# Scores of the two components side by side on the row halves of TensorE, masks behind both

## The chip, the cores and the metric

The kernel runs on one core of a Trainium2 chip. The metric is the device time of one execution in microseconds. Times of single instructions come from one profiled execution of the same program.

## The reference, cut to what matters

Two transformer blocks are computed one after the other, all in fp32, with 512 tokens and a width of 1024. The change touches only the first attention of the first block, a differential attention with 8 heads. Each head has two components of 64 features for queries and keys, and one value of 128 features:

```python
def one_block(args):                      # qblk: 128 queries, i: their block
    qblk, i = args
    s = jnp.einsum('bqhcd,bkhcd->bhcqk', qblk, k) * scale      # c: the 2 components
    causal = kpos[None, :] <= qpos[:, None]
    p = jax.nn.softmax(jnp.where(causal, s, NEG_INF), axis=-1)
    a = p[:, :, 0] - lam * p[:, :, 1]
    return jnp.einsum('bhqk,bkhe->bqhe', a, v)
```

Everything behind it (output projection, feed-forward layers, a windowed attention, a block of convolutions, another attention) is the same code before and after.

## The kernel before, in words

Each engine has its own program; they meet at counting semaphores. The first attention is the stage `heads`. It goes over 8 heads, and within a head over 4 slots, one for each block i of 128 queries. Because of the causal mask, slot i looks at n = 128 (i + 1) keys: 128, 256, 384 and 512.

In a slot TensorE does, in this order (function `slot`, L2145):

1. `scores` (L2106): for each component c one fp32 matmul of the 128 queries against n keys. Its operands stand in `da_T`, component 0 in partitions 0 to 63, component 1 in partitions 64 to 127, so that each matmul uses one half of the array's rows. It writes PSUM bank 2 + c. Behind it a bf16 matmul of the identity with a mask adds -1e30 to the part of the diagonal block that lies above the diagonal, and tells VectorE (`sc`). This one uses all 128 rows.
2. `turn` (L2122): transposes of the attention weights of the slot before, which wait for VectorE's `combine` (`comb`). In slot 3 also `turn_outputs`.
3. `project` (L2084): 24 matmuls of 384 columns, the projection of one token tile of the next head. In slot 0 it waits for that head's low weight halves (`s_lo`), which VectorE makes in `refill`.
4. `values` (L2131): the weights of the slot before times v, when ScalarE has copied them (`ate`).
5. `turn_qk` (L2098): transposes of queries and keys of one token tile, which wait for VectorE's `rope`.

VectorE goes through a slot in a fixed order: the negated row maximum of either component (`sc` to `mx`, L1685), in slot 1 the head's outputs, then `rope` of one tile of the next head (L1628 to L1634), in slots 2 and 3 more of the output's normalization, `combine` (L1643 to L1648), and last `refill` (L1675): one piece of the weights of the head after the next in slot 3, and two pieces in slot 0. ScalarE takes the exponentials (L988) behind the maxima, copies the turned weights, makes the high weight halves, and empties the projections out of PSUM.

The last head has no projection of a next head; TensorE fills its slots with steps of the output projection (L1950 to L1952), for which ScalarE (L763) and VectorE (L1305) split the weights.

Of the kernel before, what the change touches and what calls it, by code (L numbers as in the profile page):

```python
# [15 lines left out]
P = 128  # L16
D = 1024
KT_D = D // P
SEQ = 512
CTX = 256  # L20
ALL = SEQ + CTX
HD = 64
# [156 lines left out]
def program(nc, dram, out):  # L179
    stages = make_plan()  # L180
    stack = ExitStack()
    with stack:
# [3 lines left out]
        def sem(name):  # L186
            return stack.enter_context(nc.semaphore(name))
# [85 lines left out]
        pb = psum[:].rearrange("p (b n) -> p b n", b=8)  # L273
# [16 lines left out]
        s_mm = sem("block_multiplied")  # L290
# [1656 lines left out]
        def _(pe):  # L1947
# [133 lines left out]
            def heads(st):  # L2081
                S = s_da
# [23 lines left out]
                def scores(h, par, i, first):  # L2106
                    n = (i + 1) * P
                    pe.wait_ge(S["qte"], 4 * h + (i + 1))
                    qT = da_T[:, par, :]
                    for c in range(2):  # L2110
                        u = 2 * i + c
                        if not (first and i == 0):
                            pe.wait_ge(S["ex"], 8 * h + (u - 1))
                        rows_ = slice(HD * c, HD * c + HD)
                        r = pe.matmul(pb[:, 2 + c, 0:n], qT[rows_, i * P:(i + 1) * P], qT[rows_, SEQ:SEQ + n],  # L2115
                                      start=True, stop=False)
                        if u == 0:
                            r.then_inc(s_mm, 1)
                        pe.matmul(pb[:, 2 + c, i * P:n], ident_b[:], masks_b[:, 1, :], start=False, stop=True)\
                          .then_inc(S["sc"], 1)  # L2120

# [23 lines left out]
                def slot(h, par, i, first=False, more=True):  # L2145
                    j = 4 * h + i
                    scores(h, par, i, first)
                    if not more:
                        pair(st["after"], *((0, 1), (2, 3), (4, 5), (5, 6))[i])
                    if not (first and i == 0):  # L2150
                        turn(j - 1, (i - 1) % 4)
                    if not more and i < 2:
                        pair(st["after"], 2 * i + 1, 2 * i + 2)
                    if i == 3 and not first:
                        pe.wait_ge(S["qte"], j + 3 if more else 32)
                        turn_outputs(h - 1)
                    if first and i < 3:
                        project(i + 5, i + 1, 1, 1)
                    if first and i == 0:
                        turn_qk(1, 1)  # L2160
                        turn_qk(2, 2)
                    if more and not first:
                        project(j + 4, i, 1 - par, h + 1)
                    if not (first and i == 0):
                        if i == 1 and not first:
                            pe.wait_ge(S["osb"], h)
                        values(j - 1, par if i else 1 - par, (i - 1) % 4)
                    if i == 3 and not first and more:
                        pe.wait_ge(S["olo"], h)
                    if i == 0:  # L2170
                        turn_qk(j + 3, 3)
                    elif more:
                        turn_qk(j + 3, i - 1)

                for k in range(KT_D):
# [6 lines left out]
                    for t in range(4):  # L2182
# [4 lines left out]
                        r = pe.matmul(dst, xl, wh, start=False, stop=k == KT_D - 1)  # L2187
# [344 lines left out]
```

## Time and profile before

| | us |
|---|---|
| median of 3 runs | 2894.89 (2893.93 to 2895.11) |
| profiled execution, its time | 2899.06 |
| profiled execution, its span | 2897.1 |
| TensorE busy in the span | 2783.3 (96%) |
| VectorE busy | 1777.8 (61%) |
| ScalarE busy | 1115.3 (38%) |

The stage `heads` has its first scores at 41.5 us and its last at about 263.7 us. From the second head on a head takes 28.78 us. The share of busy time is one over stages with different limits, so the stage is read from its timeline. A busy TensorE also holds time in which it drains: the ends of its matmuls are modelled, and the distance from one start to the next is the surer number.

### The profile page before, as it was taken

To read this page: it belongs to the slowest core of one execution; us is meant where nothing else is said; L and a number is where in the kernel's file an instruction comes from. 1 tells how busy PE (TensorE), PEld (TensorE's weight loads), DVE (VectorE), ACT (ScalarE), POOL (GpSimd) and SP (SyncE) were. 2 spreads that over 40 slices of the span, in tenths; PEclk is the share of its full clock that TensorE was granted. 3 is DMA by queue.
4 is the path that set the end of the run, shared out by engine and by line. 5 is a ranking of instruction groups with operands and counts; after the bars stand their busy time and mean duration, and the time that the engine had idled before them with its cause. 6 is when DMAs were issued, how large, how long until landed. Compare 5 with 4: busy or idle time off the path is not lost.

```text
span 2897.1 us, 41339 instructions
## 1 busy us (share of the span) xinstructions
PE 2783.3 (96%) x14371; PEld 2317.5 (80%) x14371; DVE 1777.8 (61%) x2765; ACT 1115.3 (38%) x1869; POOL 160.5 (6%) x205
## 2 busy tenths in 40 slices
PE   7999999999788999999998999999999999999998
PEld 6887788888676788887887888888888887788886
DVE  6775667676665676667884653453456655564645
ACT  5553322224664322223433332231224666452432
POOL 5211000001110000000210000000000000000000
PEclk9999999999999999999998999999999999999999
DMA  3211355452011455532751112112111000232322
GB/s 131 65 45 58 124 179 181 165 177 75 30 37 52 145 187 175 175 131 73 158 123 45 48 64 67 59 58 69 58 57 44 15 30 30 67 101 90 100 87 66
DMA packets 75218, 263.72 MB, mean 91 GB/s; under 512 B 8496, under 2 KB 10800, under 8 KB 73264
## 3 DMA queue, kind: packets, MB, share of 16 engines
q1 hardware_dynamic: 70880, 249.99, 25.6%
q0 software_dynamic: 4176, 11.63, 2.2%
q8 instruction: 94, 1.54, 0.2%
q14 instruction: 68, 0.56, 0.1%
HBM read 247.87 MB, written 2.10 MB: 86 GB/s over the span
## 4 chain that ended last, share of the span: by engine, by line
PE 65%; issue 15%; DVE 11%; ACT 6%; DVEq 1%; ACTq 1%; POOLq 1%; POOL 0%
PE psum L1950 17%; PE psum L1951 17%; PE psum L1952 17%; DVE w_lo L1305 2%; PE psum L2115 2%; ACT work L1107 2%; DVE work L1475 1%; PE psum L2093 1%; PE psum L2095 1%; PE psum L2094 1%; PE psum L2368 1%; ACT w_hi L763 1%; ACT sw_pt L1119 1%; DVE work L1593 1%; ACT work L814 1%
## 5 line engine op out<-in xcount | busy, mean ns | idle before, releaser
L1950 PE MATMUL psum<-hx_hi,w_hi 128*128 128x512 f32 x1568 | 624.5, 398 | 4.0 <-DVE hx_lo L1587 1.2
L1951 PE MATMUL psum<-hx_lo,w_hi 128*128 128x512 f32 x1568 | 622.0, 397 | 0.0
L1952 PE MATMUL psum<-hx_hi,w_lo 128*128 128x512 f32 x1568 | 621.3, 396 | 0.0
L763 ACT ACTIVATE w_hi<-w_raw 128x1024 fp32r<-128x1024 f32 (+1 forms) x328 | 344.7, 1051 | 511.8 <-PE psum L1952 211.5
L1305 DVE TENSOR_TENSOR w_lo<-w_raw,w_hi 128x1024 fp32r<-128x1024 f32 (+1 forms) x328 | 398.2, 1214 | 197.2 <-ACT w_hi L763 179.9
L1952 PEld LDWEIGHTS psum<-hx_hi,w_lo 128*128 128x128 f32 x1568 | 295.0, 188 | 71.9
L1950 PEld LDWEIGHTS psum<-hx_hi,w_hi 128*128 128x128 f32 x1568 | 295.3, 188 | 62.8 <-DVE hx_lo L1587 4.6
L1951 PEld LDWEIGHTS psum<-hx_lo,w_hi 128*128 128x128 f32 x1568 | 295.1, 188 | 47.5
L1950 PE MATMUL psum<-a_hi,w_hi 128*128 128x512 f32 (+1 forms) x656 | 233.9, 356 | 9.5 <-DVE a_lo L1415 8.9
L1951 PE MATMUL psum<-a_lo,w_hi 128*128 128x512 f32 (+1 forms) x656 | 233.7, 356 | 0.0
L1952 PE MATMUL psum<-a_hi,w_lo 128*128 128x512 f32 (+1 forms) x656 | 233.4, 356 | 0.0
L1950 PE MATMUL psum<-o_hi,w_hi 128*128 128x512 f32 x544 | 219.4, 403 | 1.8 <-DVE w_lo L1305 1.8
L1952 PE MATMUL psum<-o_hi,w_lo 128*128 128x512 f32 x544 | 217.2, 399 | 0.0
L1951 PE MATMUL psum<-o_lo,w_hi 128*128 128x512 f32 x544 | 217.0, 399 | 0.0
L1437 DVE SCALAR_TENSOR_TENSOR work<-psum,vec,work 128x511 f32<-128x511 f32 (+1 forms) x132 | 83.2, 658 | 167.2 <-ACT work L844 158.9
L564 POOL TENSOR_TENSOR tok_r<-tok_ms,half 128x4 f32<-128x4 f32 (+1 forms) x62 | 67.2, 1084 | 1892.9 <-DVE tok_ms L1233 1581.0
L1379 DVE SCALAR_TENSOR_TENSOR X<-psum,mods,X 128x512 f32<-128x512 f32 x96 | 60.6, 659 | 173.3 <-PE psum L1952 171.1
L844 ACT ACTIVATE work<-psum,vec 128x768 f32<-128x768 f32 (+1 forms) x88 | 70.1, 797 | 225.3 <-PE psum L1952 216.8
L1950 PEld LDWEIGHTS psum<-a_hi,w_hi 128*128 128x128 f32 x656 | 124.7, 190 | 29.5 <-DVE a_lo L1415 9.5
L1952 PE MATMUL psum<-hc_hi,w_lo 128*128 128x256 f32 x512 | 144.5, 282 | 0.0
L1950 PE MATMUL psum<-hc_hi,w_hi 128*128 128x256 f32 x512 | 144.3, 282 | 0.0
L1951 PE MATMUL psum<-hc_lo,w_hi 128*128 128x256 f32 x512 | 144.0, 281 | 0.0
(310 smaller groups left out, 4920.6 us busy)
## 6 DMA issues: line engine op xcount, KB each, us to landing
mod_w<-in_w_mod SPq DMA_DIRECT2D x96, 512.0 KB, 3.8
w_raw<-in_fup SPq DMA_DIRECT2D x88, 512.0 KB, 4.6
w_raw<-in_cup SPq DMA_DIRECT2D x88, 512.0 KB, 3.6
w_raw<-in_fdown SPq DMA_DIRECT2D x32, 512.0 KB, 4.7
w_raw<-in_cdown SPq DMA_DIRECT2D x32, 512.0 KB, 3.6
sw_vb<-tap_prod POOLq DMA_DIRECT2D x29, 391.5 KB, 5.0
w_raw<-in_da_qkv SPq DMA_DIRECT2D x18, 512.0 KB, 3.6
w_raw<-in_fdown SPq DMA_DIRECT2D x16, 384.0 KB, 3.1
```

Of the source, the lines that this page charges most:

```text
L564: pool.tensor_tensor(tok_r[:, a:b], tok_ms[:, a:b], half[:, a:b], ALU.pow).then_inc(done, 1)
L763: r = act.activation(w_hi[:, off:off + n], w_raw[:, raw:raw + n], ACT.Copy)
L814: act.activation(wk[:, s % 2, 0:n], X[:, b, 0:n], ACT.Square).then_inc(s_sq, 1)
L844: act.activation(wk[:, s, 0:toks], ps_of(st, s, 0, toks), ACT.Copy, scale=vec[:, bass.ds(b + col, 1)]).then_inc(s_ctap, 1)
L1107: r = act.activation(work[:, e:e + (w1 - w0)], psum[:, w0:w1], ACT.Exp, bias=neg_max[:, col:col + 1], scale=root, accum_out=row_sum[:, col ...
L1305: r = dve.tensor_tensor(w_lo[:, off:off + n], w_raw[:, raw:raw + n], w_hi[:, off:off + n].bitcast(F32), ALU.subtract)
L1379: r = dve.scalar_tensor_tensor(X[:, b, a:e], ps_of(st, s, a, e), mods[:, l, c, bass.ds(b + o, 1)], X[:, b, a:e], ALU.mult, ALU.add)
L1437: dve.scalar_tensor_tensor(dst[:, a + 1:e], src(a, e - 1), prev, dst[:, a + 1:e], ALU.mult, ALU.add)
L1950: pe.matmul(dst, wh, xh, start=first, stop=False)
L1951: pe.matmul(dst, wh, xl, start=False, stop=False)
L1952: return pe.matmul(dst, wl, xh, start=False, stop=last)
L2115: r = pe.matmul(pb[:, 2 + c, 0:n], qT[rows_, i * P:(i + 1) * P], qT[rows_, SEQ:SEQ + n], start=True, stop=False)
```

## The change

`scores` now issues the matmuls of both components before either mask. With 384 or 512 keys each matmul is cut into two pieces of half the width, in the order component 0, component 1, component 0, component 1. `start` is set on the first piece only, which clears the bank's flags. The two masks come behind, one after the other. The waits for `ex` stand where they stood, ahead of the first piece of each component. Nothing else changes.

```diff
                     qT = da_T[:, par, :]
+                    wide = n // 2 if i >= 2 else n
+                    for a in range(0, n, wide):
+                        for c in range(2):
+                            if a == 0 and not (first and i == 0):
+                                pe.wait_ge(S["ex"], 8 * h + (2 * i + c - 1))
+                            rows_ = slice(HD * c, HD * c + HD)
+                            r = pe.matmul(pb[:, 2 + c, a:a + wide], qT[rows_, i * P:(i + 1) * P],
+                                          qT[rows_, SEQ + a:SEQ + a + wide], start=a == 0, stop=False)
+                            if i == 0 and c == 0:
+                                r.then_inc(s_mm, 1)
                     for c in range(2):
-                        u = 2 * i + c
-                        if not (first and i == 0):
-                            pe.wait_ge(S["ex"], 8 * h + (u - 1))
-                        rows_ = slice(HD * c, HD * c + HD)
-                        r = pe.matmul(pb[:, 2 + c, 0:n], qT[rows_, i * P:(i + 1) * P], qT[rows_, SEQ:SEQ + n],
-                                      start=True, stop=False)
-                        if u == 0:
-                            r.then_inc(s_mm, 1)
                         pe.matmul(pb[:, 2 + c, i * P:n], ident_b[:], masks_b[:, 1, :], start=False, stop=True)\
                           .then_inc(S["sc"], 1)
```

## Rows read from the trace of the kernel before

**Rows 1.** The page: busy time by engine over the whole span.

```profile
PE 2783.3 (96%) x14371; PEld 2317.5 (80%) x14371; DVE 1777.8 (61%) x2765; ACT 1115.3 (38%) x1869; POOL 160.5 (6%) x205
```

**Rows 2.** Stretches: length, busy time by engine, granted TensorE clock, DMA share, GB/s.

```profile
157.24:186.02 28.78, 28.78 (x163) 24.33 (x163) 21.55 (x47) 16.39 (x49) 5.83 (x6) 1.00 0.18 55
...
260.00:275.20 15.20, 13.07 (x45) 8.74 (x45) 3.68 (x7) 3.33 (x7) 0.00 (x0) 0.66 0.00 2
```

**Rows 3.** Timeline of TensorE, slot 0 of a head: start, us, instruction.

```profile
157.17 0.49 PE L2115 MATMUL psum<-da_T 64*128 64x128 f32 x2
157.59 0.23 PE L2119 MATMUL psum<-masks_b,ident_b 128*128 128x128 bf16 x1
157.75 0.48 PE L2115 MATMUL psum<-da_T 64*128 64x128 f32 x2
158.16 0.23 PE L2119 MATMUL psum<-masks_b,ident_b 128*128 128x128 bf16 x1
158.23 0.60 PE L2128 MATMUL psum<-ident,work 128*128 128x128 f32 x4
158.59 0.42 PE L2093 MATMUL psum<-w_hi,hx_hi 128*128 128x384 f32 x1
```

**Rows 4.** Timeline of TensorE: values and transposes ahead of slot 1, then slot 1.

```profile
162.91 1.05 PE L2135 MATMUL psum<-da_v,da_aT 128*128 128x128 f32 x8
163.80 0.38 PE L2103 MATMUL psum<-ident,da_qk 128*128 128x128 f32 x2
164.11 0.70 PE L2115 MATMUL psum<-da_T 64*128 64x256 f32 x2
...
165.60 0.28 PE L2128 MATMUL psum<-ident,work 128*128 128x128 f32 x1
```

**Rows 5.** Timeline of TensorE: the end of slot 1 and the scores of slot 2.

```profile
170.17 0.38 PE L2103 MATMUL psum<-ident,da_qk 128*128 128x128 f32 x2
170.48 0.91 PE L2115 MATMUL psum<-da_T 64*128 64x384 f32 x2
...
172.39 0.39 PE L2128 MATMUL psum<-ident,work 128*128 128x128 f32 x2
```

**Rows 6.** Timeline of TensorE: the scores of slot 3.

```profile
177.62 1.12 PE L2115 MATMUL psum<-da_T 64*128 64x512 f32 x2
178.67 0.23 PE L2119 MATMUL psum<-masks_b,ident_b 128*128 128x128 bf16 x1
178.83 1.12 PE L2115 MATMUL psum<-da_T 64*128 64x512 f32 x2
...
179.95 0.50 PE L2128 MATMUL psum<-ident,work 128*128 128x128 f32 x3
```

**Rows 7.** Timeline of VectorE in slot 3, idle time before in brackets.

```profile
178.94 0.69 DVE L1685 TENSOR_REDUCE neg_max<-psum 128x1 f32<-128x512 f32 x1 [1.32 <-PE psum L2119]
180.16 0.69 DVE L1685 TENSOR_REDUCE neg_max<-psum 128x1 f32<-128x512 f32 x1 [0.52 <-PE psum L2119]
...
185.79 1.22 DVE L1675 TENSOR_TENSOR w_lo<-w_raw,w_hi 128x1024 fp32r<-128x1024 f32 x1 [0.16 <-issue]
```

**Rows 8.** Timeline of VectorE: refill in slot 3, rope in slot 1, first maximum in slot 2.

```profile
157.01 1.23 DVE L1675 TENSOR_TENSOR w_lo<-w_raw,w_hi 128x1024 fp32r<-128x1024 f32 x1 [0.16 <-issue]
...
169.01 0.42 DVE L1634 TENSOR_TENSOR da_qk<-work,tok_r 128x256 f32<-128x256 f32 x1
...
171.59 0.56 DVE L1685 TENSOR_REDUCE neg_max<-psum 128x1 f32<-128x384 f32 x1 [1.04 <-PE psum L2119]
```

**Rows 9.** Timeline of all engines in the last head, slots 2 and 3.

```profile
257.36 1.02 DVE L1685 TENSOR_REDUCE neg_max<-psum 128x1 f32<-128x384 f32 x2
...
259.51 0.71 PE L2135 MATMUL psum<-da_v,da_aT 128*128 128x128 f32 x4 [1.38 <-ACT da_aT L960]
...
260.15 1.38 PE L2115 MATMUL psum<-da_T 64*128 64x512 f32 x2
...
261.68 2.07 PE L2115 MATMUL psum<-da_T 64*128 64x512 f32 x2
```

## Prediction

> **What bounds the kernel now.** I read the page first: TensorE is busy for 96% of the span [rows 1], so the question is whether it also sets the pace where the change is, and what in its busy time is not streaming. The change touches only the stage `heads`. By stretches, a head takes 28.78 us there, TensorE has no idle time in it and its full clock, VectorE is busy for 21.5 us and ScalarE for 16.4 [rows 2]. So TensorE sets the pace of the middle heads, and VectorE comes next. It is next by more than its share says, since its work is in a fixed order; two of its deadlines are close, and I come to them below.
>
> Then TensorE's timeline, by distances from start to start. In slot 0 the first scores start at 157.17, their mask 0.42 later, the second scores 0.16 behind the mask, and the first transpose 0.07 behind the second mask: 1.06 us in all [rows 3]. In slot 3 the same distances are 1.05, 0.16, and 1.12 for the second pair, 2.33 in all [rows 6]. 384 more columns cost 0.63 us a matmul, 1.65 ns a column. So 128, 256, 384 and 512 keys stream for 0.21, 0.42, 0.63 and 0.84 us a component, and 0.20 us between scores and mask belong to no column. Nor does most of the 0.16 behind a mask: where the next instruction also uses all rows, it comes 0.07 behind it [rows 3]. Each change from half of the rows to all and back thus costs 0.20 + 0.09, about 0.30 us, and a slot has two such round trips. Slots 1 and 2 fit: 1.49 and 1.91 us [rows 4, 5] against 0.85 and 1.27 of streaming and 0.64 of the rest.
>
> **The change part by part.** *Masks behind both.* One of two round trips goes: 0.30 us a slot, if going from one half of the rows to the other costs nothing. No row shows such a step. I take nothing; the bound above is a full round trip, 0.30 a step.
>
> *Components next to each other.* No row shows two matmuls on different halves either. Lower bound: nothing, they stream one behind the other. Upper bound: both stream at once and half of the columns' time goes. I take a value between these. Four loads (0.44) then bind in slot 0, and eight (0.88 for 5/8 of 1.27, 0.79) in slot 2.
>
> New slot lengths, with 0.20 to the mask, 0.06 to the second mask and 0.06 to what follows:
> - slot 0: 0.44 + 0.32 = 0.76, saves 0.30
> - slot 1: 3/4 of 0.85 is 0.63, + 0.32 = 0.95, saves 0.54
> - slot 2: 0.88 + 0.32 = 1.20, saves 0.71
> - slot 3: 5/8 of 1.69 is 1.06, + 0.32 = 1.38, saves 0.95
>
> That is 2.5 us a head. *Waits.* Those for `ex` ask for exponentials of the slot before, taken some 5 us earlier; component 1's now stands between pieces and still finds them done.
>
> *Pieces.* They add two matmuls with four loads to slots 2 and 3. The loads are in the sums above. Without the overlap they lie under passes of 0.16 and 0.21 us, longer than 0.11, and I cost them at nothing; with that cover gone it would be 0.44 in each of them.
>
> The Trainium skill (TensorE: Matmul & The Clock Gate, "Part 3: Packing small matmuls") says that matmuls on different row groups run at the same time with starts some 4 ns apart, and measured 3.07 times for four of them. Taken whole it would give full pairing, the second rival below; no row here shows it.
>
> *What VectorE gives back.* Its maximum of component 0 now waits for both components. In slot 3 the two maxima start 1.32 and 2.54 us behind the scores [rows 6, 7], the first 0.27 behind its mask. New: 1.06 + 0.20 + 0.27 = 1.53 for the first, and some 0.60 behind it the second (back to back, two of 384 columns take 1.02 [rows 9], and one of 512 takes 0.69 [rows 7]): 2.13, only 0.41 earlier, while TensorE saves 0.95. From there VectorE has work without a break to its refill, which ends 9.39 us behind the scores of slot 3 [rows 6, 7]. The projection of slot 0 waits for it, and starts only 0.35 us behind its end [rows 3, 8]. After the change the refill ends at 8.98, the projection can start at 9.03, and without it TensorE would be there at 9.74 - 0.95 - 0.30 = 8.49. It waits 0.54: slots 3 and 0 save 0.71 together, not 1.25.
>
> The second deadline: from that refill's end rope's last instruction of slot 1 ends 11.19 us later [rows 8], and the transposes that wait for it start 11.58 behind the projection [rows 3, 5]. With 0.54 saved TensorE is there at 0.05 + 11.04 and VectorE at 11.19 + 0.05: it waits 0.15, and slot 1 saves 0.39. Ahead of its first maximum VectorE had idled 1.04 us in slot 2 and 1.32 in slot 3 [rows 7, 8], so slot 2 keeps its 0.71. Sum for a middle head: 0.71 + 0.39 + 0.71 = 1.81 us.
>
> ScalarE's exponentials follow the maxima and are no later than they; its 16.4 us of 28.78 leave room. The weights' DMAs are let go by `wlo`, and their share is 0.18 [rows 2]; they stay hidden.
>
> **The sum.** Six periods from slot 3 to slot 3: 6 x 1.81 = 10.9. Slots 0 to 2 of the first head, which have no refill deadline ahead of them: 0.30 + 0.54 + 0.71 = 1.5. Slot 3 of head 6 and slot 0 of head 7: 0.95 + 0.30 = 1.2. Slots 1 and 2 of head 7: nothing, since there the chain goes through weight splits on ScalarE and VectorE; the maxima of slot 2 start at 257.36, and TensorE later waits 1.38 us for ScalarE [rows 9]. Slot 3 of head 7 falls where the granted clock is 0.66 on average, a mix of 1.2 and 2.4 GHz [rows 2], and its scores take 1.38 and 2.07 us for 1.12 [rows 6, 9]: between 0.95 and twice that, I take 1.4. Total 15.0 us. Behind the stage TensorE again sets the pace (96% busy over the span), and nothing there is reordered, so it is shifted whole.
>
> The profiled execution took 2899.06 us with a span of 2897.1, 4.2 us over the median of 2894.89, so its durations are good to 0.15%; the saving is taken from the median: 2880. I take 0.2%, 5.8 us, as what a measurement can tell from no change.
>
> **The rivals.**
> - *In one mode, but one behind the other.* For it: matmuls start in program order in all rows, and no row shows overlap. Then a slot saves 0.30, but in slot 3 the maxima come at 1.69 + 0.20 + 0.27 = 2.16 and 2.76, 0.22 later, so the refill's deadline takes nearly all of slots 3 and 0: 9.61 + 0.05 against 9.74, 0.08 saved. A middle head saves 0.68, six 4.1, the rest 1.9: 6 us, 2889. Against it: the operands lie on disjoint partitions and the outputs in different banks. Chance 0.23, half of it inside 0.2%.
> - *Full pairing.* Both components stream at once. Slot 3 has its first maximum at 0.84 + 0.47 = 1.31, which saves 0.22 more per middle head in the refill's deadline; slots 1 and 3 change little behind deadlines, slot 2 gains 0.2 more. Some 0.45 x 6, and 0.5 at the ends: 18 us, 2877. Two passes on the same rows and program order speak against it. By the Trainium skill's page above this is the rule; it would move the forecast by 3 us. Chance 0.10.
> - *VectorE doesn't bind* (its order has more slack than I read): 6 x 2.5 + 4.1 = 19 us, 2876. Within the first case's chance.
> - *Each step from half to half drains the array* (the other side). Place: between the pieces; one step in slots 0 and 1, three in slots 2 and 3. With d us a step, a middle head loses 7d (1 + 3 + 3; slot 3 through the maxima), all slots some 54d, against the 6 us of the first rival. Zero is at d = 0.11, 5.8 us slower from d = 0.22; with the 0.30 of a whole round trip it is 6 - 16 = -10 us, 2905. For it: going from half to all rows does cost 0.20. The Trainium skill (TensorEngine Tiling, "Key Properties") says that changing the mode drains and changing the tile does not; no row here shows the second. Chance 0.10.
> - *The clock falls.* TensorE's new waits (0.54 and 0.15 a head) are shorter than the 1.38 us ahead of the half-clock stretch [rows 2, 9]. Chance of a net loss by it, or of anything else, 0.05.
>
> **How the numbers follow.** The forecast's own case has 0.52 and lies between 2876 and 2884. With full pairing 0.10, that is 0.62 clearly faster; of the serial rival half (0.12) too: 0.74 faster. Same: the other half, 0.11, half of the drain case with small d, and part of the rest: 0.17. Slower: 0.09. The range goes from 2874 (full pairing, nothing bound by VectorE) to 2891 (the serial rival with its own uncertainty); drains lie outside.
>
> **What would show it.** In the new trace: a middle head of 26.97 us; slot 3's scores to the first transpose 1.38 us, slot 0's 0.76; the second component's scores starting before the first's second pass has ended; TensorE idle before L2093 in slot 0 for VectorE's w_lo, some 0.5 us a head. Wrong would be: scores of 2.0 us and more in slot 3 (serial), gaps between pieces (drain), or a head near 26.3 (VectorE no bound).

## The result

| | before | after |
|---|---|---|
| median, us | 2895.00 (4 runs, 2893.93 to 2895.28) | 2875.21 (4 runs, 2867.96 to 2877.07) |
| profiled execution, span | 2897.1 | 2872.2 |
| from first scores to last scores | 218.7 | 203.0 |
| from last scores to first projected output | 26.3 | 20.6 |

The ratio is 0.9926, with a 95% interval of 0.9911 to 0.9941: 17 to 26 us less, where 15 were forecast. Taken from the median of before that is 2873.5 us, half a microsecond under the range (the medians themselves differ by 19.8). The sign was right and so was the stage; the size was too small. On another chip the same kernel had 0.9937 (0.9923 to 0.9952).

The page after. TensorE has lost 31 us of busy time, the other engines next to nothing.

```profile
PE 2752.5 (96%) x14435; PEld 2306.5 (80%) x14435; DVE 1775.2 (62%) x2765; ACT 1112.8 (39%) x1869; POOL 159.6 (6%) x205
```

TensorE's timeline after: the scores of slots 3, 0 and 1 of a middle head, with the masks, the first transpose, and the first projection of slot 0 (start, us, instruction, idle time before).

```profile
166.04 1.13 PE L2116 MATMUL psum<-da_T 64*128 64x256 f32 x8
167.11 0.28 PE L2121 MATMUL psum<-masks_b,ident_b 128*128 128x128 bf16 x2
167.23 0.50 PE L2130 MATMUL psum<-ident,work 128*128 128x128 f32 x3
...
173.23 0.49 PE L2116 MATMUL psum<-da_T 64*128 64x128 f32 x4
173.65 0.28 PE L2121 MATMUL psum<-masks_b,ident_b 128*128 128x128 bf16 x2
173.77 0.60 PE L2130 MATMUL psum<-ident,work 128*128 128x128 f32 x4
174.89 0.44 PE L2093 MATMUL psum<-w_hi,hx_hi 128*128 128x384 f32 x1 [0.51 <-DVE w_lo L1675]
...
180.43 0.70 PE L2116 MATMUL psum<-da_T 64*128 64x256 f32 x4
181.06 0.28 PE L2121 MATMUL psum<-masks_b,ident_b 128*128 128x128 bf16 x2
181.19 0.28 PE L2130 MATMUL psum<-ident,work 128*128 128x128 f32 x1
```

Read against [rows 3, 4, 6]: from the first scores to the first mask it was 0.42 us in slot 0 and 1.05 in slot 3 for one component. Now it is 0.42 and 1.07 for both. The second component costs at most 0.02 us. The slots take 0.54, 0.76, 0.98 and 1.19 us for 1.06, 1.49, 1.91 and 2.33. And the projection of slot 0 now waits for VectorE's `w_lo`, which had been early. The 0.51 us in the row are counted from the modelled end of the transposes. By starts the wait is longer: the projection came 9.74 us behind the scores of slot 3 before and comes 8.85 behind them now, and slots 3 and 0 alone, 1.14 and 0.52 us shorter, would bring it to 8.08. So it is held back by 0.77 us.

VectorE after, in slot 3 and behind it:

```profile
167.38 1.29 DVE L1685 TENSOR_REDUCE neg_max<-psum 128x1 f32<-128x512 f32 x2 [0.93 <-PE psum L2121]
...
173.61 1.23 DVE L1675 TENSOR_TENSOR w_lo<-w_raw,w_hi 128x1024 fp32r<-128x1024 f32 x1 [0.16 <-issue]
175.08 0.49 DVE L1685 TENSOR_REDUCE neg_max<-psum 128x1 f32<-128x128 f32 x2 [0.25 <-issue]
```

The first maximum starts 1.34 us behind the scores and the refill ends 8.80 behind them (173.61 + 1.23 - 166.04), 0.05 ahead of the projection. Before it was 1.32 and 9.39 [rows 6, 7].

What TensorE waited for in the heads, after (total, times, longest):

```profile
PE psum L2093 <- DVE w_lo L1675: 2.8, 6, 0.6
...
PE psum L2103 <- DVE da_qk L1634: 1.1, 3, 0.6
```

The first deadline of the forecast, the refill's, is met late six times. The second, rope's in slot 1, is among the other three only once, in head 3, but by starts it shows in heads 2 and 4 too, where slot 1 is 5.78 us long for 5.64 in head 5. The longest of the three is none that the forecast priced. It stands in head 6, slot 2, where VectorE splits a piece of the output projection's weights ahead of its maxima and so comes late to rope:

```profile
214.18 1.23 DVE L1305 TENSOR_TENSOR w_lo<-w_raw,w_hi 128x1024 fp32r<-128x1024 f32 x1 [1.76 <-ACT w_hi L763]
215.49 1.02 DVE L1685 TENSOR_REDUCE neg_max<-psum 128x1 f32<-128x384 f32 x2
...
218.92 0.44 PE L2103 MATMUL psum<-ident,da_qk 128*128 128x128 f32 x2 [0.56 <-DVE da_qk L1634]
```

That slot takes 7.13 us, as long as before the change (7.14), where slot 2 of the other middle heads went from 7.13 to 6.19. The six periods, 27.19, 26.42, 26.91, 26.43, 26.22 and 27.03 us, are not alike.

The other part of the surprise is in the last head. The stretch of 15 us that was granted 0.66 of the clock [rows 2], a mix of 1.2 and 2.4 GHz, is at its full clock, 2.4 GHz, after (stretches: length, busy time by engine, clock, DMA share, GB/s):

```profile
240.00:244.00 4.00, 1.69 (x14) 1.21 (x12) 2.97 (x7) 1.51 (x5) 0.00 (x0) 1.00 0.36 131
244.00:252.00 8.00, 5.82 (x38) 4.62 (x35) 3.17 (x6) 3.00 (x7) 0.00 (x0) 1.00 0.00 0
```

The first projected output, before and after, ends the exit:

```profile
286.46 0.69 DVE L1376 TENSOR_TENSOR X<-psum,X 128x512 f32<-128x512 f32 x1 [3.43 <-PE psum L1952]
```

```profile
263.78 0.69 DVE L1376 TENSOR_TENSOR X<-psum,X 128x512 f32<-128x512 f32 x1 [3.44 <-PE psum L1952]
```

So the saving by stretches, from the two timelines (starts of first instructions, before and after), against the forecast:

| stretch | before | after | saved | forecast |
|---|---|---|---|---|
| first scores to slot 3 of head 0 | 21.09 | 18.94 | 2.2 | 1.5 |
| six periods, slot 3 of head 0 to slot 3 of head 6 | 172.60 | 160.19 | 12.4 | 10.9 |
| to slot 3 of head 7 | 24.97 | 23.85 | 1.1 | 1.2 |
| from there to the first projected output | 26.31 | 20.64 | 5.7 | 1.4 |
| sum | | | 21.4 | 15.0 |

The two spans also differ by 1.3 us ahead of the first scores and by 2.2 behind the stage. The part behind the stage took 2599 to 2611 us in the profiles of this study, with the same code, so I read nothing into these.

### The profile page after: what moved, and what is told of

The parts are those of the page before. It is cut to its first block, busy times and chain, and to the rows that moved or that the text cites. A ratio compares the mean times of both kernels' runs of the same rounds, so it can differ in the third digit from the quotient of the medians.

```text
span 2872.2 us, 41467 instructions
## 1 busy us (share of the span) xinstructions
PE 2752.5 (96%) x14435; PEld 2306.5 (80%) x14435; DVE 1775.2 (62%) x2765; ACT 1112.8 (39%) x1869; POOL 159.6 (6%) x205
## 4 chain that ended last, share of the span: by engine, by line
PE 62%; issue 15%; DVE 13%; ACT 6%; DVEq 2%; ACTq 1%; POOLq 0%; POOL 0%
PE psum L1950 17%; PE psum L1951 17%; PE psum L1952 17%; DVE w_lo L1305 2%; DVE work L1475 2%; ACT work L1107 2%; PE psum L2370 1%; ACT w_hi L763 1%; PE psum L2093 1%; PE psum L2094 1%; PE psum L2095 1%; ACT sw_pt L1119 1%; DVE work L1593 1%; ACT work L814 1%; DVE neg_max L1838 1%
```

## The experiments

"Changed kernel" is the one after. "Exit" is the time from the last scores to the first projected output, a period that from slot 3 of one head to slot 3 of the next.

### Without pieces

```diff
-                    wide = n // 2 if i >= 2 else n
+                    wide = n
```

> The components next to each other, but no pieces: each matmul keeps its full width. Theory A (the two halves of the array stream at once whatever the cut): the scores of slots 2 and 3 take 0.98 and 1.19 us to the next transpose, as in the changed kernel, and the time is the changed kernel's within 0.1%. Theory B (the forecast's: one pass of four stands alone, pieces shrink it): slot 3 takes about 1.6 us, slot 2 about 1.3, and the time is about 3 to 5 us above the changed kernel's.

Slot 3 of a middle head, TensorE's timeline of this kernel:

```profile
139.76 1.13 PE L2116 MATMUL psum<-da_T 64*128 64x512 f32 x4
140.82 0.29 PE L2121 MATMUL psum<-masks_b,ident_b 128*128 128x128 bf16 x2
```

1.06 us to the mask, as with pieces; periods the same within 0.05 us; ratio to before 0.9934 (0.9913 to 0.9955). Theory A holds. The pieces change nothing, and the picture in which the first pass of four stands alone is wrong.

### Both components on one half

```diff
-                            rows_ = slice(HD * c, HD * c + HD)
+                            rows_ = slice(0, HD)
```

> As the changed kernel, but component 1's matmuls read component 0's rows as well (so the second component's result is left out): both stand on the same half of the array, the order, the pieces and the number of mode changes stay. Theory A (overlap of the halves is most of the gain): slot 3 takes 0.84 us more, 2.03 us, slot 0 0.75, VectorE's maxima come later, and the time is near the serial rival's, 5 to 7 us under the kernel before, so some 15 us above the changed kernel. Theory B (the gain is that two mode changes went, and pieces on one half cost nothing more): within 5 us of the changed kernel.

```profile
146.43 1.99 PE L2116 MATMUL psum<-da_T 64*128 64x256 f32 x8
148.36 0.28 PE L2121 MATMUL psum<-masks_b,ident_b 128*128 128x128 bf16 x2
...
154.47 0.71 PE L2116 MATMUL psum<-da_T 64*128 64x128 f32 x4
155.11 0.28 PE L2121 MATMUL psum<-masks_b,ident_b 128*128 128x128 bf16 x2
```

1.93 and 0.64 us to the mask: 0.86 and 0.22 more than the changed kernel. That is the streaming of the second component, 0.84 and 0.21 by the columns. The ratio is 0.9972 (0.9959 to 0.9985), 8 us under before; forecast for the serial rival were 6. Theory A, then. Against 0.9926 and 0.9934 with the halves side by side, the pairing is worth some 11 to 13 us by the ratios. By the two profiles, from first scores to first projected output, it is 15 us, 3.6 of them in the exit, where this kernel's clock fell and the changed kernel's did not. The masks behind both components give the rest.

### Pieces only

```diff
-                        r = pe.matmul(pb[:, 2 + c, 0:n], qT[rows_, i * P:(i + 1) * P], qT[rows_, SEQ:SEQ + n],
-                                      start=True, stop=False)
-                        if u == 0:
-                            r.then_inc(s_mm, 1)
+                        wide = n // 2 if i >= 2 else n
+                        for a in range(0, n, wide):
+                            r = pe.matmul(pb[:, 2 + c, a:a + wide], qT[rows_, i * P:(i + 1) * P],
+                                          qT[rows_, SEQ + a:SEQ + a + wide], start=a == 0, stop=False)
+                            if u == 0:
+                                r.then_inc(s_mm, 1)
```

> The kernel before, with the scores of slots 2 and 3 cut in two pieces and each mask behind its own component. Theory A (the loads of the added pieces lie under the passes): slots 2 and 3 stay 1.91 and 2.33 us, the time stays within 0.1%. Theory B (each added load stands open, 0.11 us): slots 2 and 3 grow by 0.44 us each, 5 to 7 us in all.

Ratio 1.0005 (0.9991 to 1.0018), periods 28.79 us for 28.78. Theory A: the added loads cost 0.01 us a head.

### The third refill piece in slot 2

```diff
-        FIRST_REFILL, REFILL = ((), (0,), (1,), (2,)), ((0, 1), (), (), (2,))
+        FIRST_REFILL, REFILL = ((), (0,), (1,), (2,)), ((0, 1), (), (2,), ())
```

> The changed kernel, with the third refill piece moved from slot 3 to slot 2 on ScalarE and VectorE. Theory A (TensorE waits in slot 0 for that piece, 0.47 us in each of six heads): the wait is gone, a middle head goes from 26.4 to about 25.9 us, 2 to 3 us less in all, if rope's deadline in slot 1 is met too. Theory B (VectorE's order is full all through, the lateness only moves to slot 3): no change within 0.05%.

The six periods take 156.3 us in place of 160.2, and the waits for `w_lo` fall from 2.8 to 0.2 us; three new ones for `combine`'s weights (L1648) are there, 0.8 us in all. Mechanism A holds inside the heads. The time does not show it: 0.9926 (0.9906 to 0.9945), and this profile's exit is 22.0 us, since the clock was at half for 3.4 us, from 0.3 us behind the start of its last scores.

### The same edit on the kernel before

The same line is changed, in the kernel before.

> The kernel before, with the third refill piece moved from slot 3 to slot 2. Theory A (before the change TensorE alone set the pace, VectorE's refill was 0.35 us early): a head stays 28.78 us and the time the same within 0.1%. Theory B (the move itself helps or hurts ScalarE's or the DMAs' order): more than 2 us either way.

Periods 28.78 us, ratio 0.9995 (0.9986 to 1.0003). VectorE's refill was no bound before the change. The change made it one.

### One refill piece in each of slots 0, 1 and 2

```diff
-        FIRST_REFILL, REFILL = ((), (0,), (1,), (2,)), ((0, 1), (), (), (2,))
+        FIRST_REFILL, REFILL = ((), (0,), (1,), (2,)), ((0,), (1,), (2,), ())
```

> The changed kernel with VectorE's and ScalarE's refill pieces in slots 0, 1 and 2, one each, in place of two in slot 0 and one in slot 3. Theory A (VectorE's two deadlines, the refill before slot 0's projection and rope in slot 1, are all that keeps a middle head at 26.4 us): the head goes to 25.5 us, the sum of TensorE's own slots, 5 to 6 us less in all than the changed kernel. Theory B (other waits stand behind them): the head stays above 25.8.

Theory B: other waits stand behind them. A head does not only stay above 25.8 us, the periods grow to 26.7 to 27.4. TensorE's waits in this kernel:

```profile
PE psum L2103 <- DVE o_lo L1664: 2.1, 4, 0.5
PE psum L2130 <- DVE work L1648: 1.3, 5, 0.3
...
PE psum L2093 <- DVE w_lo L1675: 0.2, 1, 0.2
```

All but 0.2 us of the wait for `w_lo` is gone and two others are there. Against the version with the third piece in slot 2, a piece went from slot 0 to slot 1, and that brought the 2.1 us for `o_lo`, at the end of slot 3 in four heads. The ratio, 0.9932 (0.9916 to 0.9948), can't be told from the changed kernel's on the same chip.

### The changed kernel again

> The changed kernel once more, to stand beside the next ones on one chip, and for a second profile of its last head. Theory A (the clock in the last head is the changed kernel's own: its scores and waits keep TensorE from falling to half clock there): the stretch of 15 us that was granted 0.66 before is near 1.00 again, and this gives 3 to 4 us of the gain each time. Theory B (chance of one execution): it is low in this profile, and the time from the last scores to the first projected output is as long as in the kernel before.

0.9937 (0.9923 to 0.9952), periods as in the first profile within 0.03 us, exit 20.64 us at full clock again: Theory A by its numbers.

### Masks ahead of the scores

The added lines:

```diff
+                    for c in range(2):
+                        if not (first and i == 0):
+                            pe.wait_ge(S["ex"], 8 * h + (2 * i + c - 1))
+                        r = pe.matmul(pb[:, 2 + c, i * P:n], ident_b[:], masks_b[:, 1, :], start=True, stop=False)
+                        if i == 0 and c == 0:
+                            r.then_inc(s_mm, 1)
+                    for c in range(2):
+                        rows_ = slice(HD * c, HD * c + HD)
+                        r = pe.matmul(pb[:, 2 + c, i * P:n], qT[rows_, i * P:(i + 1) * P],
+                                      qT[rows_, SEQ + i * P:SEQ + n], start=False, stop=True)
+                        if i == 0:
+                            r.then_inc(S["sc"], 1)
+                    for c in range(2):
+                        if i:
+                            rows_ = slice(HD * c, HD * c + HD)
+                            pe.matmul(pb[:, 2 + c, 0:i * P], qT[rows_, i * P:(i + 1) * P], qT[rows_, SEQ:SEQ + i * P],
+                                      start=False, stop=True, skip_group_check=True).then_inc(S["sc"], 1)
```

> The changed kernel with both masks ahead of the scores (start set on the mask), the diagonal block's columns and the others as two matmuls a component, halves next to each other. The number of mode changes in a slot is the same. Theory A (the halves pair fully in any order and a maximum can start as soon after scores as after a mask): the first maximum of slot 3 starts 1.3 us behind the first instruction of the group, as now, a head is as long, the time is within 0.1% of the changed kernel. Theory B (the drain of 0.20 us ahead of the masks is off VectorE's path then): the maxima come 0.2 us earlier, six deadlines move, 1 to 2 us less.

Slot 3 in this kernel, TensorE and VectorE:

```profile
167.62 0.28 PE L2113 MATMUL psum<-masks_b,ident_b 128*128 128x128 bf16 x2
...
168.90 0.55 PE L2134 MATMUL psum<-ident,work 128*128 128x128 f32 x3
169.00 1.29 DVE L1685 TENSOR_REDUCE neg_max<-psum 128x1 f32<-128x512 f32 x2 [0.97 <-PE psum L2125]
```

The first maximum starts 1.38 us behind the first mask, against 1.34 behind the first scores. The 0.20 us were not saved but moved: they now stand between the masks and the scores, and the slot is 1.28 us long for 1.19. The six periods are as in the changed kernel, 0.9931 (0.9914 to 0.9948). Theory A.

### The new order in one slot only, and in all but one

Both orders stand in the kernel, and one slot takes the other:

```diff
+                def scores(h, par, i, first):
+                    last = isinstance(h, int) and h == 7 and i == 3
+                    (scores_grouped if last else scores_apart)(h, par, i, first)
```

> The kernel before in all slots but one: only slot 3 of the last head has its components next to each other with the masks behind. Theory A (what lets the clock fall to half in the last head is that slot's 2.1 us of scores on one half of the array after the other): the fall is gone, last scores to first projected output take about 21 us for 26.3, and the time is 4 to 6 us under the kernel before by this one slot. Theory B (the fall comes from what lies ahead of that slot, or from where the slots stand in time): the clock still falls, 1 us less at most.

> A second look at the kernel before with the new order in slot 3 of the last head alone. Theory A: full clock and 20.6 us from the last scores to the first projected output again. Theory B: a fall as in the kernel before, 25 us.

Each second look of this kind is one execution, read for its timeline alone. One slot of 32 in the new order: the exit goes from 26.31 to 20.64 us in the first profile and 20.63 in the second, with full clock. The ratio is 0.9979 (0.9968 to 0.9990), 6 us (3 to 9) for this slot alone, of which 1.1 is its own streaming and round trip. Theory A. The granted clock around the last scores, in the kernel before (scores from 260.15) and in this one (from 259.88):

```profile
257.00:261.00 4.00, 2.62 (x12) 1.49 (x11) 2.99 (x7) 1.51 (x5) 0.00 (x0) 0.99 0.42 131
261.00:265.00 4.00, 4.00 (x8) 1.73 (x8) 1.39 (x2) 1.04 (x3) 0.00 (x0) 0.50 0.00 0
```

```profile
258.00:262.00 4.00, 2.76 (x18) 2.13 (x19) 2.59 (x7) 1.25 (x6) 0.00 (x0) 1.00 0.38 127
262.00:266.00 4.00, 2.38 (x16) 1.77 (x15) 1.89 (x5) 2.34 (x6) 0.00 (x0) 1.00 0.00 0
```

The other way round:

```diff
-                    (scores_grouped if last else scores_apart)(h, par, i, first)
+                    (scores_apart if last else scores_grouped)(h, par, i, first)
```

> The changed kernel in all slots but one: slot 3 of the last head has the old order. Theory A: the fall is back, last scores to first projected output take about 26 us, and the time is 4 to 6 us above the changed kernel, some 13 to 15 under the kernel before. Theory B: the clock stays up, and only that slot's own 1.1 us is lost.

> A second look at the changed kernel with the old order in slot 3 of the last head. Theory A (that slot's order decides on the clock): last scores to first projected output near 26 us and half clock around those scores again. Theory B (the first look's fall, which began ahead of that slot's scores, was chance): near 21.8 us, the changed kernel's 20.6 and 1.1 for the slot.

The ratio is 0.9943 (0.9931 to 0.9955), which can't be told from the changed kernel's 0.9926 and 0.9937: the 4 to 6 us of Theory A are not shown in the time. The clock fell both times, but not at the same place. First profile, stretches of 1 us, then second profile, TensorE's timeline:

```profile
242.00:243.00 1.00, 0.00 (x0) 0.00 (x0) 0.82 (x3) 1.00 (x5) 0.00 (x0) 0.88 0.87 311
243.00:244.00 1.00, 0.85 (x4) 0.85 (x4) 0.85 (x3) 0.10 (x1) 0.00 (x0) 0.50 0.50 193
```

```profile
243.15 0.71 PE L2157 MATMUL psum<-da_v,da_aT 128*128 128x128 f32 x4 [2.31 <-ACT da_aT L960]
243.79 1.12 PE L2115 MATMUL psum<-da_T 64*128 64x512 f32 x2
...
245.01 1.31 PE L2115 MATMUL psum<-da_T 64*128 64x512 f32 x2
246.26 0.29 PE L2119 MATMUL psum<-masks_b,ident_b 128*128 128x128 bf16 x1
```

In the first it had fallen before the last scores began (at 244.30), behind a wait of 2.3 us; the exit is 27.2 us. In the second it fell during them, and the exit is 23.2, between the two theories.

### The kernel before again, and one half in the last slot

> A second profile of the kernel before. Theory A: 26.3 us and a granted clock near 0.66 for 15 us, as in the first. Theory B: it can also stay at full clock, with 21.8 us.

Exit 26.33 us, the same fall.

```diff
-                            rows_ = slice(HD * c, HD * c + HD)
+                            rows_ = slice(0, HD) if isinstance(h, int) and h == 7 and i == 3 else slice(HD * c, HD * c + HD)
```

> The changed kernel, but in slot 3 of the last head component 1's matmuls read component 0's rows (its result is left out there), so that this slot's scores stand on one half of the array one behind the other, 0.86 us longer. Theory A (a long stretch on half of the array at this place lets the clock fall): half clock behind these scores, 24 us or more from them to the first projected output. Theory B (masks between the components, or chance): full clock and 21.5 us.

Exit 25.2 us, so Theory A by its number. But here too the clock had fallen ahead of the scores, 1.2 us before their start, at the end of a wait of 2.3 us.

### What the runs point to

The changed kernel without pieces and with the third refill piece in slot 2.

> The version that the runs so far point to: components next to each other, no pieces, third refill piece in slot 2. Six periods of a head take 156.3 us, 3.9 less than the changed kernel's 160.2. Theory A (that comes through): 0.9925 or less of the kernel before. Theory B (it is eaten by a part fall of the clock in the last head, as in the version with pieces): within 0.1% of the changed kernel.

Theory A. Six periods 157.1 us, exit 20.63 at full clock, 2871.67 us median, ratio 0.9911 (0.9898 to 0.9925). It is the fastest of all here. Over the changed kernel it gains 3 us in the profile's heads; the intervals overlap, so that the time alone does not prove it.

## Why the forecast was too small

**The pace of the stage.** Right. TensorE set it in the heads before, and a slot's saving showed there as far as VectorE's deadlines let it: the periods that end in heads 2 and 4 are 26.42 and 26.43 us for 28.78, some 2.35 saved of the 3.32 by which the scores of four slots are shorter.

**VectorE's deadlines.** The mechanism was right, and it ate most of that error: the slots' scores are 0.82 us a head shorter than forecast, 4.9 over six periods, but the six periods only 1.5 (12.4 saved for 10.9). The refill's end was forecast 8.98 us behind slot 3's scores and came at 8.80; the second rival has 8.76. The wait was forecast as 0.54, by starts, and by starts it is 0.77, since TensorE would be there 0.41 earlier than forecast; that the row shows 0.51 is no hit. Rope's wait was forecast as 0.15 and is 0.14 in heads 2 and 4. Two terms are missing in 6 x 1.81: the weight splits of head 6, and VectorE's 0.62 us of idle time in head 3, shown in the last section. The periods with them are 27.03 and 26.91 us for the 26.22 to 26.43 of the others behind the first. Moving the refill gives back 3.9 us over six periods, 3.0 without pieces, and nothing in the kernel before. So this part of the difference is 1.5 us in all.

**The last head.** This is the largest mis-sized term: 1.4 us forecast, 5.7 measured, 4.3 of the 6.4 us between forecast and profile. Of the 5.7, the slot's own scores at full clock are 1.1. This step failed too: I priced only the last slot's scores at the clock that the rows showed, and took the fall of the clock as one that the change leaves as it is. It does not. Over all profiles of this study, by what stood in the last slot:

| last slot | profiles | exit, us |
|---|---|---|
| old order | before twice, pieces only, refill on before, all but last twice | 26.3, 26.3, 26.3, 26.3, 27.2, 23.2 |
| one half, one behind the other | both on one half, last on one half | 24.3, 25.2 |
| halves side by side | the nine others | 20.6 to 20.7 eight times, 22.0 once |

With the other slots in the old order, pieces and refill either way, the order of this one slot goes with the fall: the clock fell in all four profiles with the old order in it, 0.65 to 0.84 us behind the start of the last scores, and in neither of the two with the new one, behind the same wait of 1.4 us. The time shows it as well, with 6 us. With the other slots in the new order it is not shown. There the wait ahead of the slot is 2.3 us. All three fell that had the last slot's scores one behind the other, but in two of them (the first look at all but last, and last on one half) the clock was down 1.5 and 1.2 us before the slot began, which no later instruction can have caused; and one of the seven with the halves side by side fell too, 0.3 us behind the slot's start and for 3.4 us. The kernel with both components on one half fell as well, behind a wait of 1.7 us. What starts a fall, and whether the side by side slot prevents it or only ends it sooner, stays open.

**The rivals.** Serial streaming: out, by the run without overlap and its 0.64 and 1.93 us. Full pairing: right in its mechanism; its 2877 is 3.5 us above the result, since it has the forecast's last head. VectorE doesn't bind: out, by its late refills. Clock: the rival had the wrong sign; with the new waits the granted clock stays at 1.00 from 72 us to the end of the stage in both profiles of the changed kernel.

## What to carry to other kernels

Two fp32 matmuls with 64 rows each, on different halves of the array and in different banks, cost as much as one here, and without cutting them. Put them next to each other and keep full-height matmuls out from between. Then look at once for the engine that was next, by its deadlines and not by its busy share, head by head; here one line moved a piece of its work and gave 0.5 to 0.65 us a head back. Where a clock fall stands in the profile of before, take its whole length as a term that the change may give back or bring, not only the instructions that you touch.

## What the runs showed of the hardware that was not expected

- Two fp32 matmuls on the two row halves streamed at once: 0.42 us to the mask for one and for two at 128 columns, 1.05 and 1.07 at 512.
- The weight loads of the two halves do not add up either. On all rows eight loads with passes of 128 columns took 0.89 us [rows 4]; on one half four of each took 0.44 (0.64 to the mask less 0.20); on two halves 0.22.
- Ahead of its first maximum in the head that begins the second pass of the loop over heads, VectorE is idle for 0.62 us, where it is 0.20 to 0.25 in heads 2, 4 and 5. In the kernel before the idle time was as long, but hidden. The row is in the changed kernel, in head 3, whose rope in slot 1 then comes late by 0.6 us; the period around it is 26.91 us for 26.42:

```profile
122.12 0.49 DVE L1685 TENSOR_REDUCE neg_max<-psum 128x1 f32<-128x128 f32 x2 [0.62 <-issue]
```
